# Moving the weight buffers and activations of an fp32r kernel to 1 KB multiples within a partition

## What is computed

```
for l in range(2):
    h = rmsnorm(x, g_mix_pre[l])
    mk, mv = split(rmsnorm(mem, g_mem[l]) @ w_mem_kv[l])
    main, mq = mlstm_mixer(h, ...) if l == 0 else swa_mixer(h, ...)
    mo = memory_attention(mq, mk, mv)
    x = x + rmsnorm(concat(main, mo) @ w_out[l], g_mix_post[l])
    gate, up = split(rmsnorm(x, g_ffn_pre[l]) @ w_ffn_in[l])
    x = x + rmsnorm((silu(gate) * up) @ w_ffn_out[l], g_ffn_post[l])
```

## The kernel before

| tensors | first byte | past a multiple of 1 KB |
|---|---|---|
| raw, whi, wlo | 16512, 32896, 49280 | 128 |
| K (constants, 5760 bytes) | 65664 | 128 |
| V, gpost, small | 71424, 71872, 75968 | 768, 192, 192 |
| H, XR, R and all overlaid in them | 78016, 110784, 127168 | 192 |

## Time and profile before

### The profile page before, as it was taken

One profiled execution on the slowest core, in us unless ns is written; L12 is line 12 of the kernel. 1 busy time (PEld: TensorE's weight loads), 2 busy tenths in 40 slices (PEclk: granted clock), 3 DMA queues, 4 the chain that ended last, 5 costly groups with the idle time before them and its releaser, 6 DMA issues.

```text
span 2001.5 us, 32809 instructions
## 1 busy us (share of the span) xinstructions
PE 1968.7 (98%) x13488; PEld 1781.3 (89%) x13488; DVE 1145.0 (57%) x1595; ACT 932.6 (47%) x1647; POOL 145.5 (7%) x149
## 2 busy tenths in 40 slices
PE   8999999999999999999999999999999999999998
PEld 6798888877889778888999899999988799999998
DVE  3375347465343233353353999972377659999523
ACT  4443142355433342355454755652258856565422
POOL 0000000000000000000000233300000003333000
PEclk9999999999999999999999999999999999999999
DMA  6521122211334123332212233332231113223331
GB/s 179 146 85 64 43 84 84 85 64 59 111 112 162 63 106 105 106 116 89 81 48 80 77 125 106 106 126 95 97 116 43 64 64 116 106 106 106 127 106 64
DMA packets 29824, 191.24 MB, mean 96 GB/s; under 512 B 3689, under 2 KB 4841, under 8 KB 8562
## 3 DMA queue, kind: packets, MB, share of 16 engines
q1 hardware_dynamic: 26562, 178.58, 25.4%
q0 software_dynamic: 3120, 10.62, 2.0%
HBM read 185.38 MB, written 3.67 MB: 94 GB/s over the span
## 4 chain that ended last, share of the span: by engine, by line
PE 90%; DVE 5%; ACT 3%; issue 1%; DMA 1%; SPq 0%; DVEq 0%; ACTq 0%
PE PS L561 21%; PE PS L563 20%; PE PS L562 20%; PE PS L1034 6%; PE PS L1036 6%; PE PS L1035 6%; DVE wlo L2721 1%; ACT whi L1546 1%; PE PS L895 1%; PE PS L714 1%; PE PS L731 1%; PE PS L1152 1%; PE PS L917 1%; PE PS L851 1%; PE PS L1344 1%
## 5 line engine op out<-in xcount | busy, mean ns | idle before, releaser
L2323 DVE TENSOR_TENSOR wlo<-raw,whi 128x2048 fp32r<-128x2048 f32 (+2 forms) x117 | 264.9, 2264 | 375.3 <-ACT whi L1546 374.9
L1546 ACT ACTIVATE whi<-raw 128x2048 fp32r<-128x2048 f32 (+2 forms) x250 | 311.7, 1256 | 211.1 <-PE PS L563 190.7
L561 PE MATMUL PS<-hhi,whi 128*128 128x512 f32 (+1 forms) x768 | 313.2, 408 | 3.1 <-DVE hlo L2370 3.0
L563 PE MATMUL PS<-hhi,wlo 128*128 128x512 f32 (+1 forms) x768 | 302.7, 394 | 0.0
L562 PE MATMUL PS<-hlo,whi 128*128 128x512 f32 (+1 forms) x768 | 301.3, 392 | 0.0
L561 PE MATMUL PS<-whi,ahi 128*128 128x256 f32 x704 | 196.1, 279 | 0.0
L562 PE MATMUL PS<-wlo,ahi 128*128 128x256 f32 x704 | 196.1, 279 | 0.0
L563 PE MATMUL PS<-whi,alo 128*128 128x256 f32 x704 | 196.1, 278 | 0.0
L561 PEld LDWEIGHTS PS<-hhi,whi 128*128 128x128 f32 (+1 forms) x768 | 144.4, 188 | 40.7 <-DVE hlo L2370 5.4
L1034 PE MATMUL PS<-shi,whi 128*128 128x256 f32 x640 | 179.5, 280 | 0.9 <-DVE gated_ L2766 0.4
L1036 PE MATMUL PS<-shi,wlo 128*128 128x256 f32 x640 | 178.5, 279 | 0.0
(11 more groups left out here) (458 smaller groups left out, 4605.8 us busy)
## 6 DMA issues: line engine op xcount, KB each, us to landing
raw<-in_stream SPq DMA_DIRECT2D x165, 1024.0 KB, 4.8
gpost<-in_gposts POOLq DMA_DIRECT2D x5, 512.0 KB, 7.6
X<-in_x SPq DMA_DIRECT2D x4, 512.0 KB, 6.1
X<-in_x POOLq DMA_DIRECT2D x1, 2048.0 KB, 10.4
out<-X SPq DMA_DIRECT2D x4, 512.0 KB, 2.6
bias_line<-linet POOLq DMA_DIRECT2D x1, 1536.0 KB, 35.1
tbias<-bias_line POOLq DMA_DIRECT2D x1, 1024.0 KB, 7.5
memx<-in_mem POOLq DMA_DIRECT2D x1, 1024.0 KB, 5.4
```

Source lines behind the costliest of these rows:

```text
L561: nc.tensor.matmul(out, lh, rh, start=(k == 0), stop=False)
L563: return nc.tensor.matmul(out, ll, rh, start=False, stop=(k == n_k - 1))
L1546: return nc.scalar.activation(out_, in_, func, scale=scale)
L2323: V_.tensor_tensor(wlo[:, s % 2, :, cols_], raw[:, s % 2, :, cols_], whi[:, s % 2, :, cols_], ALU.subtract)\
```

## The change

`K` is given out first, then 256 bytes that nothing uses (`to_kb`), then the weight buffers; `V`, `gpost` and `small` move behind the regions.

```
+TO_KB = 64
...
+        K = sb("K", [P, K_ALL])
+        sb("to_kb", [P, TO_KB])
         raw = sb("raw", [P, 2, KT, C])
         whi = sb("whi", [P, 2, KT, C], F32R)
         wlo = sb("wlo", [P, 2, KT, C], F32R)
-        K = sb("K", [P, K_ALL])
-        V = sb("V", [P, V_COLS])
-        gpost = sb("gpost", [P, D])
-        small = sb("small", [P, 512])
...
+        V = sb("V", [P, V_COLS])
+        gpost = sb("gpost", [P, D])
+        small = sb("small", [P, 512])
```

## The result

The changed kernel takes 2024.76 us (median of four runs, 2021.75 to 2026.19), the kernel before 2001.82 in the same comparison. The ratio is 1.0121, with a 95% interval of 1.0104 to 1.0138. The forecast of no change was wrong, and so was its range.

A forecast was written before the change was run, and what follows sets the result against it. TensorE, busy 98% of the span, was taken to bound the kernel. TensorE, ScalarE, VectorE and DMA terms summed to 0 on 2001.5 us; likeliest time 2000 us, own range 1996 to 2006, wider range 1968 to 2011.

The forecast's parts named there:

- The forecast of no change: Whole kernel: time stays within 1996 to 2008 us, with 2000 as its middle; chance 0.42.
- The step that failed: TensorE's fp32r matmuls: addresses don't pick between the 113.3 and 117.8 ns paces, so aligning starts changes zero.
- The ends of the range: Whole span: -112 - 2.6 us if fp32r matmuls ran like plain fp32, +12.4 + 2.6 us if all went long.
- Rival C: TensorE: aligned, equal offsets lock 256-column matmuls into the long pace; 12.4 us more, 2014 us; chance 0.20.
- 512 columns: TensorE's 2,928 matmuls of 512 moving columns: zero taken, 5.6 us less if they fall to 226.7 ns.
- Rivals A and B: TensorE, aligned: A keeps the short pace, middle 1980 us, chance 0.29; B drops a 1 KB-boundary cost, 1890 us, 0.09.
- The gap of N/2.4 + 2.5: TensorE matmul starts: the skill's 109.2 and 215.8 ns; if alignment were what is missing, 1901 us.
- ScalarE, VectorE and DMA at zero: Roundings and slot loads beside TensorE: no change, with ends of 1.6 us and 1 us either way.
- rival A: TensorE keeps the short pace, but the first FFN products may wait for VectorE, leaving 12.3 us not won; chance 0.29.
- The phase idea: TensorE: phase between weight-load and moving streams, set anew at each stall, picks the pace; largest single flip 6.6 us.

The follow-up runs named there:

- e1: Changed kernel's tensor order, but weights at 128 and activations at 192 within 1 KB, as in the kernel before: 2000.2 us, ratio to before 0.9995.
- e3: Changed kernel with 64 bytes between wlo and H: weights at 1 KB multiples, activations 64 past: 1999.32 us, ratio to before 0.9992.
- e7: Kernel before with the first FFN product's split sums 128 bytes further, so weights start 64 past the sums: 2003.58 us, ratio 1.0003.
- e8: Kernel before with region H moved to distance 0 from the weights, R and XR left at 64: 2001.32 us, ratio 0.9998.
- e6: Changed kernel with 192 bytes between wlo and H, turning round the distance's sign of the kernel before: 2013.99 us, ratio to before 1.0065.
- m1: Separate kernel of fp32r matmuls alone, pairs of moving and stationary starts within 1 KB: 120.0 ns at equal starts for 256 columns.
- m4: Matmuls alone, 256 columns, distance 64 or 192, one matmul of 0 to 512 columns ahead: short in 72 and 13 of 104 starts.
- m2: Matmuls alone, moving start 0, stationary start at every 64 bytes to 960, some groups with other engines busy: 120.0 ns at 0, 256, 512, 768.
- m3: Matmuls alone, distances in 16-byte steps and unequal low and high distances: of 14 distances only 64 gave 113.3 ns, others 116.5 to 120.3.
- e2: Against the changed kernel, weights and activations both start 192 past a 1 KB multiple, distance still 0: 2026.76 us, ratio to before 1.0144.
- e5: Changed kernel with 256 bytes between wlo and H, distance 256 in both forms of product: 2025.58 us, ratio to before 1.0118.

## Why the prediction was wrong

**The step that failed** is "I take zero. The nearest rows are those of one product at both paces with the same offsets, and they say that the address is not the switch." They show that the address doesn't fix the pace between 113.3 and 117.8. They don't show that another distance has the same two. All rows of before had a distance of 64 bytes to one side or the other; I had no row at 0 and read a variation at one point as independence from the variable. The stationary starts at 128 and 640 or 192 and 704, which I took as a test, differ by 512, two whole periods of 256, so they tested nothing. All 8,736 matmuls of 256 columns then averaged 119.94 ns, a third pace that no row of before had.

**What the rows of before held unread.** Products that move weights (+64) and products that move activations (-64) stood side by side in the earlier trace rows. At 604 us the stretch with the long pace (585 to 603) passes into the one with the short pace (605 to 623), and just there the matmuls change from moving `cmhi` and `cmlo` against the weights to moving the weights against them. No gap between starts there is over 123 ns. The same step from 117.8 to 113.3 ns at the same place is in e1, e3, e7 and e8, with e6's signs turned round it is 113.3 on both sides, and after the change 120.0. So besides a wait, the change of the distance itself moved the pace. The prediction pooled both forms.

**The ends of the range** came from the paces seen before and its far end from plain fp32. Rival C named the right condition, two streams at equal offsets, but expected the long pace of before, so its price was bounded by 117.8 ns. Measured is a mean of 119.94. Against the mean of 116.39 that is 3.55 ns x 8,736 = 31.0 us, where C had 12.4. "Nothing is slower than 118.2" was no argument, as no row had that distance. C's condition for being right, a pace over 119, came true.

**512 columns** were priced at zero with a gain of 5.6 us as the end. The gain came, 1.94 ns x 2,928 = 5.7 us, but that the size fits is luck: the prediction tied it to 256-column matmuls that all go short, and they all went long.

**Rivals A and B** are refuted: the short pace is gone, no stretch is under 119, and e3, with one operand aligned, is as fast as before but no faster. The excess over plain fp32 is not a cost of 1 KB boundaries, since absolute starts of 0, 64, 128 and 192 all give 120.0 at equal offsets (m1).

**The gap of N/2.4 + 2.5.** The Trainium skill, TensorE: Matmul & The Clock Gate, "Back-to-back issue gap", gives this formula (109.2 and 215.8 ns) for a single matmul by itself, and for a stream of weight loads and matmuls a lower figure, about 131 ns at 512 columns. I had held the formula against streams, which it isn't given for. The groups of m1 to m4, which are such streams, have 113.3 and 226.7 ns as their lowest, so for fp32r the trace disagrees with the figure for streams, and none comes down to the formula either.

**ScalarE, VectorE and DMA at zero** were right for the roundings, the remainders and the slot loads; VectorE's sums of weight quarters took 5.5 us more, while VectorE as a whole took 0.8 less. That TensorE meets fewer waits for VectorE when it is slower I had priced only in the other direction, in rival A; it is in the 9.2 us given back, as argued above.

**The phase idea** was half right: there is a draw at a start and a pace that then holds, shown in m2 and m4, but only at some distances, and +64 was short more often in m4 (72 of 104 against 13 of 104), m1 and m3, though not in m2. In the profiled execution of before, weights-moving products were short in 45% of their matmuls and the others in 13%. e6 with the sign turned round has 25% and about half. The share at +64 is 27% for the weights-moving products of e7 and 55% for those of e3, so one execution tells little about it. Untested is whether the draw also accounts for all of the spread between executions: with 64 bytes the kernel before ranged from 1992.7 to 2011.6 us in 23 runs, with 0 the four runs of e2 lay within 1.1 us, those of e5 within 2.8 and those of the changed kernel within 4.4.

## What to carry to other kernels

In a stream of fp32r matmuls that each load new weights, look at where the moving and the stationary operand start relative to one another within 256 bytes, not at whether they are aligned. Equal starts were among the worst for 256 columns (120.0 ns) and the best for 512 (226.7); 64 bytes apart gave 113.3 or 117.8 and, depending on the sign, 229 or 233. So weigh the two lengths by their counts, and when a trace has only one value of a variable, measure another before pricing it at zero.

## What the runs showed that I had not expected

- The pace of fp32r matmul and weight load pairs depends on the distance of their starts with a period of 256 bytes, in kernels where TensorE works almost alone. That two reads get into each other's way is the natural reading, and no run here looks inside it.
- At +64 and -64 there are two steady paces 4.4 ns apart with the same addresses, drawn at the start of a group; in the whole kernel one such pace held for over 150 us.
- 16 bytes matter: 512 columns take 226.7 ns at -16 and 233.3 at -32.
